# Post-norms by token at four stage boundaries of a two-block transformer kernel, with four weight slots

## The chip, the cores and the metric

The kernel runs on one core of a Trainium2 chip. The metric is the device time of one execution in microseconds (us). The core has TensorE (PE in the profile; PEld is its weight load), VectorE (DVE), ScalarE (ACT) and GpSimd (POOL); SyncE (SP) only sends DMAs. The engines run their own instruction lists in order and meet at semaphores.

## The reference, cut to what matters

512 tokens of width 1024 go through two blocks. The first block is four steps, each with a norm before and a norm after:

```
h = h + 0.5*rmsnorm(swiglu(rmsnorm(h, g1), Wg, Wu, Wd), p1)     # FFN 1, inner width 2816
h = h +     rmsnorm(token_mixer(rmsnorm(h, g2)), p2)            # mixer, ends in y @ w_o
h = h + 0.5*rmsnorm(swiglu(rmsnorm(h, g3), Wg', Wu', Wd'), p3)  # FFN 2
gate = sigmoid(rmsnorm(h, g4) @ w_gate);  e = p @ w_proj        # e has an inner width of 256
h = h +     rmsnorm(gate * e, p4)
rmsnorm(x, g) = x * rsqrt(mean(x*x) + 1e-6) * g                 # mean over the 1024 features
```

The second block starts with `rmsnorm(h, norm_mix_2) @ w_in_2`, then has three mixers (a short convolution, sparse attention with 6 heads, dilated attention with 6 heads), a projection, a gated addition and a last norm.

## The kernel before, in words

**Layout.** `h` lies with features on the partitions: eight tiles `hs[k]` of 128 features by 512 tokens. So do `xh` and `xl`, the operands of the next stage: every factor of a large product is split in a high part (rounded) and a low part (the rest), and a product is three matmuls, `hi*hi`, `hi*lo` and `lo*hi`. `ACT` makes a high part by a copy, `DVE` the low part by a subtraction.

**Weights.** They are read once, in 261 units of mostly 128x1024 numbers (512 KB). SP sends a unit into slot `j % SLOTS` of `raw`; ACT writes `whi` from it (`split_hi`), DVE writes `wlo = raw - whi` (`split_lo`), PE reads `whi` and `wlo`. There are `SLOTS = 3` of each of the three. SP waits for `w_lo` of unit j-3 before it sends unit j. `ahead(n)`, which `along` calls at each unit of a group in ACT's and DVE's lists, splits up to unit n+2 (`AHEAD = 2`).

**Products.** A group (`("ffn1", "gu", g)`, `("v", c)`, `("dv",)` and so on) fills four PSUM banks `G[0..3]`. `gemm` goes unit by unit (two k-tiles), in each unit bank by bank, six matmuls for each. With `by_token` a bank holds 128 tokens by up to 512 features (x is the stationary operand); else it holds 128 features by 512 tokens. One unit is 24 matmuls. `pumps` and `hooks` put small work of other kinds between two banks of a unit: attention steps (`background`) or the sums of a norm.

**A boundary (p1 after FFN 1, p2 after the mixer, p3 after FFN 2, p4 after the gate).** The last group of a stage leaves f with features on the partitions. `post_square` squares the eight tiles on ACT, POOL adds the first four, PE sums over the partitions with a column of ones (`total`, `post_sums`), ACT takes the root and DVE the reciprocal, both write a diagonal matrix (`diagonal`), and PE spreads it over the partitions (`spread`) into bank `X[1]`. Only then can `next_input` run: for each of the eight tiles DVE computes `f = f*gain*X[1]` and `h = h + f`, ACT `xh = h*gain` and a square of h, DVE `xl`. The next group's matmuls for k-tile m wait for `x_lo` of tile m. The pre-norm factor of the next stage is not multiplied into x. It is computed from the squares of h (POOL adds them, `pre_gather`), summed on PE at hook `(6, 0)` of the next stage's first group and applied when the banks are read out. At p3 one unit of another group (`("pp", 0)`) lies between the sums and `next_input`.

**Attention.** In the second block the single-tile units (`tiles_in`) are interleaved with attention steps: after each k-tile pair one `pump`. For pair n of a head and a query block the steps are: PE scores, DVE `score` (maximum), ACT exp, DVE `scale` (multiply by the weight), PE `turn_p` (transposes), ACT and DVE copy into `ptr`, PE `weigh`. In DVE's list the order of a round is copy of n, `score(n + 2)` (in the dilated part n + 4), then after a `yield` `scale(n + 1)`. At the end of a unit DVE's and ACT's lists hold reading out the bank (`store`), activations and the split of the next weight unit.

Of the kernel before, what the change touches and what calls it, by code (L numbers as in the profile page):

```python
# [17 lines left out]
SLOTS = 3  # L18
# [95 lines left out]
def two_blocks(nc, A, out):  # L114
    ctx = ExitStack()
    with ctx:
# [51 lines left out]
        rows, _ = sb("rows", [104, 128], F32)  # L168

# [4 lines left out]
        emb = at("emb", [128, 4, T], F32, ah_o)  # L174
        wsr = at("wsr", [128, 4, 128], F32, bh_o)
        xrow = f[:, :, :].rearrange("p k t -> p (k t)").rearrange("p (i c) -> p i c", i=4)
        vtok = xrow
# [52 lines left out]
        sum_done, spread_done, prep_mm = signal("sum_done"), signal("spread_done"), signal("prep_mm")  # L230
        sgu_done, pooled_done = signal("sgu_done"), signal("pooled_done")
# [5 lines left out]
        pt_act, od_done = signal("pt_act"), signal("od_done")  # L237
# [3 lines left out]
        pt_dve, post_done = signal("pt_dve"), signal("post_done")  # L241
# [53 lines left out]
        for name, c in (("pp", 0), ("pg", 0), ("pg", 1), ("pp", 1)):  # L295
            halves(name, *((A["ple_w_proj"][0], 2) if name == "pp" else (A["ple_w_gate"][0], KD)), 0, (c,))
# [81 lines left out]
        def along(group, tiles, ahead, background=None, pumps=(), hooks=None):  # L378

            first, nk, _ = plan[group]  # L380
            for u in range(0, nk, 2):
# [48 lines left out]
        x0_after = {"p1": "s0", "s1": "p1", "p2": "s1", "s2": "p2", "p3": "s2", "s3": "p3", "p4": "s3", "s4": "p4"}  # L430

        def tensor(pe):
# [3 lines left out]
            def gemm(group, x, tiles, by_token=False, order=None, pumps=(), hooks=None, ks=None):  # L436
                first, nk, wid = plan[group]
                order = order or list(range(tiles))
                for u in range(0, nk, 2):
                    n = first + u // 2  # L440
                    kn = min(2, nk - u)
                    pe.wait_ge(w_lo, n)
                    for ti, m in enumerate(order):
                        for kk in range(kn):
                            hi, lo, key = x[ks[u + kk] if ks else u + kk]
                            wv = [w[:, n % SLOTS, kk * wid:(kk + 1) * wid] for w in (whi, wlo)]
                            if u + kk == 0:
                                for s, v in g_free[m]:
                                    pe.wait_ge(s, v)
                            pe.wait_ge(x_hi, key)  # L450
                            for wi, xv in ((0, hi), (1, hi), (0, lo)):
                                start = u + kk == 0 and wi == 0 and xv is hi
                                stop = u + kk == nk - 1 and xv is lo
                                if xv is lo:
                                    pe.wait_ge(x_lo, key)
                                if by_token:
                                    t = pe.matmul(G[m][:, 0:wid], xv[:, m * 128:(m + 1) * 128], wv[wi], start, stop)
                                else:
                                    t = pe.matmul(G[m][:, :], wv[wi][:, m * 128:(m + 1) * 128], xv, start, stop)
                                if stop:  # L460
                                    t.then_inc(*acc_done.event((group, m)))
                                elif xv is lo and kk == kn - 1 and ti == tiles - 1:
                                    t.then_inc(*unit_read.event(n))
                        if ti in pumps:
                            pump(background)
                        if hooks and (u, ti) in hooks:
                            hooks[u, ti]()
# [9 lines left out]
            def total(st, j, sq, first=False, end=False):  # L477
                if first and st in x0_after:
                    pe.wait_ge(rooted, x0_after[st])
                for i in range(4):  # L480
                    t = pe.matmul(X[0][:, i:i + 1], sq[:, i * 128:(i + 1) * 128], ones[:, 0:1], first and i == 0,
                                  end and i == 3)
                t.then_inc(*sum_done.event((st, j)))

            def spread(st, slot):
                pe.wait_ge(diag_dve, st)
                pe.wait_ge(diag_act, st)
                for i in range(4):
                    t = pe.matmul(X[1][:, i * 128:(i + 1) * 128], ones[:, :], sqs[slot][:, i * 128:(i + 1) * 128], True, True)
                t.then_inc(*spread_done.event(st))  # L490

            def pre_hooks(st):
                def sums():
                    pe.wait_ge(const, "ones")
                    pe.wait_ge(summed, (st, 7))
                    total(st, "acc", acts[3], True, True)

                def factor():
                    spread(st, 0)
                return {(6, 0): sums, (6, 2): factor}  # L500

            def post_hooks(st):
                def sums():
                    pe.wait_ge(summed, (st, 3))
                    total(st, "acc", acts[0], True)
                return {(6, 0): sums}

            def post_sums(st):
                for j in range(4, KD):
                    pe.wait_ge(squared, (st, j))  # L510
                    total(st, j, sqs[j % 2] if j < 6 else acts[j - 5], False, j == KD - 1)
# [25 lines left out]
            def ffn(name, x, st, post, hooks, pumps=(), fill=None):  # L537
                for hf, (g0, g1) in enumerate(GROUPS):
                    for g in range(g0, g1):
                        gemm((name, "gu", g), x, 4, order=[0, 2, 1, 3], pumps=pumps if g else (),  # L540
                             hooks=hooks if g == 0 else None)
                        g_free[:] = [[(scaled, (name, g, m))] for m in range(4)]
                    for c in range(2):
                        gemm((name, "dn", hf, c), HT[name, hf], 4, hooks=post_hooks(post) if hf and c else None)
                        g_free[:] = [[(taken if hf == 0 else f_scaled, (name, hf, 4 * c + m))] for m in range(4)]
                if fill:
                    fill()
                else:
                    post_sums(post)
                    spread(post, 0)  # L550
# [16 lines left out]
            ffn("ffn1", XT["x0"], "s0", "p1", hooks, (3,))  # L567


            for c in range(2):  # L570
                gemm(("v", c), XT["x1"], 4, by_token=True, hooks=pre_hooks("s1") if c == 0 else None)
# [61 lines left out]
            for c in range(2):  # L633
                gemm(("wo", c), AT["y"], 4, hooks=post_hooks("p2") if c else None)
                g_free[:] = [[(f_scaled, ("wo", 4 * c + m))] for m in range(4)]
            post_sums("p2")
            pe.wait_ge(mixed, ("sgu", 6))
            spread("p2", 0)


# [10 lines left out]
            def project():  # L651
                def rest():
                    post_sums("p3")

                def along_it():
                    spread("p3", 0)
                gemm(("pp", 0), PT["p"], 4, hooks={(0, 0): rest, (0, 3): along_it})
                g_free[:] = [[(taken, ("emb", m))] for m in range(4)]

            background.append(embed("p", None))  # L660
            ffn("ffn2", XT["x2"], "s2", "p3", pre_hooks("s2"), (3,), project)


            gemm(("pg", 0), XT["x3"], 4, pumps=(1, 3), hooks=pre_hooks("s3"))
            drain(background)
            g_free[:] = [[(scaled, ("pg", m))] for m in range(4)]
            gemm(("pg", 1), XT["x3"], 4, pumps=(1, 3), hooks=post_hooks("p4"))
            g_free[:] = [[(scaled, ("pg", 4 + m))] for m in range(4)]
            gemm(("pp", 1), PT["p"], 4, pumps=(3,))
            g_free[:] = [[(f_scaled, ("pg", 4 + m))] for m in range(4)]  # L670
            post_sums("p4")
            spread("p4", 0)


            gemm(("dv",), XT["x4"], 4, by_token=True, hooks=pre_hooks("s4"))
# [195 lines left out]
            for t_no, (name, m, n) in enumerate(tiles_in):  # L871
# [6 lines left out]
                for k in range(KD):  # L878
                    hi, lo, key = XT["x4"][k]
# [22 lines left out]
            def sums():  # L902
                pe.wait_ge(summed, ("fin", 3))
                pe.wait_ge(exp_done, (PAIRS - 1, 1))
                total("fin", "acc", acts[0], True)
# [19 lines left out]
        def scalar(act):  # L925
# [19 lines left out]

            def start_hi(k):
# [7 lines left out]
            def pre_square(st, m):  # L954

                if m >= 3:
                    act.wait_ge(summed, (st, m - 2))
                square(st, m, hs[m], sqs[m % 2] if m else acts[3])
# [4 lines left out]

            def diagonal(st):
                act.wait_ge(r_done, st)
                for i in (1, 3):
                    t = act.activation(sqs[0][:, i * 128:(i + 1) * 128], ident[:, :], ACT.Copy, scale=rtok[:, i:i + 1])
                t.then_inc(*diag_act.event(st))
# [5 lines left out]
            def pre_hooks(st):  # L974
                def sums():
                    act.wait_ge(const, "eps")
                    root(st, "acc")
                    diagonal(st)
# [14 lines left out]
            def factors(st):  # L993
                root(st, 7)
                diagonal(st)

            def next_input(st, x, gain, between=None):

                for m in range(KD):
                    act.wait_ge(h_done, (x[m][2][0], m))  # L1000
                    act.activation(x[m][0], hs[m], ACT.Copy, scale=col(gain, m)).then_inc(*x_hi.event(x[m][2]))
                    pre_square(st, m)
                    if m == 0 and between:
# [1184 lines left out]
```

## Time and profile before

| | |
|---|---|
| median of 3 runs (lowest, highest) | 1699.48 us (1697.94, 1704.07) |
| the profiled execution, own time | 1704.4 us |
| its span, first to last instruction | 1702.5 us |
| PE busy | 1631.2 us, 96% |
| PEld, DVE, ACT, POOL busy | 78%, 45%, 34%, 12% |
| mean granted TensorE clock | 0.969 |

PE is busy nearly all the time, but its busy time holds stretches at the lower clock and small matmuls too, so the stretches in which it is not at full work have to be looked up one by one.

### The profile page before, as it was taken

How to read it: one execution, taken by the hardware profiler on the slowest of the kernel's cores; microseconds unless marked ns; L12 is line 12 of the kernel's file. 1: busy time of each engine (PE TensorE's matmuls, PEld its weight loads, DVE VectorE, ACT ScalarE, POOL GpSimd, SP SyncE). 2: the span in 40 equal slices, each digit the busy share in tenths (PEclk: the TensorE clock that was granted, in tenths of full speed). 3: DMA queues.
4: the chain of work that ended last, by engine and by line, in shares of the span. 5: the costliest groups of instructions: out<-in, count | busy, mean ns of one | idle time of the engine just before them, and what ended most of it. 6: DMA issues, size and time to landing. Idle time of an engine off the chain costs nothing.

```text
span 1702.5 us, 19182 instructions
## 1 busy us (share of the span) xinstructions
PE 1631.2 (96%) x7926; PEld 1321.6 (78%) x7926; DVE 765.3 (45%) x1055; ACT 575.7 (34%) x866; POOL 211.3 (12%) x193
## 2 busy tenths in 40 slices
PE   8999999998999999998999999998989998987998
PEld 6778888887888778887888888886878676665787
DVE  5444234437444433447444234427464534555444
ACT  5223222325332332234333223324443413333333
POOL 2311001102023200122111001102040000001100
PEclk9999999998999999997999999998989998998999
DMA  5322333231323223231333333221244221211231
GB/s 162 124 88 98 100 99 99 91 96 62 99 75 100 79 83 99 98 106 49 97 97 100 99 99 94 93 98 38 83 105 100 49 53 25 50 38 37 82 105 50
DMA packets 123605, 144.59 MB, mean 85 GB/s; under 512 B 18768, under 2 KB 86496, under 8 KB 123520
## 3 DMA queue, kind: packets, MB, share of 16 engines
q1 hardware_dynamic: 122096, 138.57, 26.4%
q0 software_dynamic: 1424, 4.82, 1.1%
q8 instruction: 62, 1.02, 0.2%
q14 instruction: 23, 0.19, 0.0%
HBM read 141.26 MB, written 2.10 MB: 84 GB/s over the span
## 4 chain that ended last, share of the span: by engine, by line
PE 89%; DVE 7%; ACT 2%; issue 1%; DMA 0%; SPq 0%; DVEq 0%; ACTq 0%
PE G L57 79%; PE X L57 7%; DVE wlo L69 1%; PE X L60 1%; DVE xl L72 1%; DVE h L69 1%; DVE f L72 1%; PE G L60 1%; ACT whi L63 1%; DVE stat L78 1%; ACT prb L63 0%; DVE prb L75 0%; DMA f<-in_x_dram 0%; DVE tmp_t L69 0%; DVE act_t L69 0%
## 5 line engine op out<-in xcount | busy, mean ns | idle before, releaser
L69 DVE TENSOR_TENSOR wlo<-raw,whi 128x1024 fp32r<-128x1024 f32 (+2 forms) x261 | 320.9, 1232 | 584.1 <-ACT whi L63 583.8
L57 PE MATMUL G<-xh,whi 128*128 128x512 f32 x1304 | 525.9, 403 | 14.9 <-ACT emb L63 3.4
L57 PE MATMUL G<-xl,whi 128*128 128x512 f32 x1304 | 513.8, 394 | 1.5 <-DVE xl L72 1.4
L57 PE MATMUL G<-xh,wlo 128*128 128x512 f32 x1304 | 513.9, 394 | 0.0
L63 ACT ACTIVATE whi<-raw 128x1024 fp32r<-128x1024 f32 (+2 forms) x261 | 270.5, 1039 | 583.1 <-PE G L57 575.9
L57 PEld LDWEIGHTS G<-xh,whi 128*128 128x128 f32 x1304 | 248.9, 191 | 73.0 <-issue 16.8
L57 PEld LDWEIGHTS G<-xl,whi 128*128 128x128 f32 x1304 | 248.2, 190 | 56.9 <-DVE xl L72 3.7
L57 PEld LDWEIGHTS G<-xh,wlo 128*128 128x128 f32 x1304 | 248.9, 191 | 48.0
L57 PE MATMUL G<-ah,whi 128*128 128x512 f32 x448 | 176.6, 394 | 1.1 <-issue 1.1
L57 PE MATMUL G<-al,whi 128*128 128x512 f32 x448 | 174.4, 389 | 0.0
L57 PE MATMUL G<-ah,wlo 128*128 128x512 f32 x448 | 174.3, 389 | 0.0
L69 POOL TENSOR_TENSOR tmp_t<-tmp_t,act_t 128x512 f32<-128x512 f32 x52 | 72.5, 1398 | 590.9 <-ACT act_t L63 482.6
L69 POOL TENSOR_TENSOR act_t<-act_t,sq_t 128x512 f32<-128x512 f32 x50 | 74.6, 1492 | 341.0 <-ACT sq_t L63 339.0
L57 PEld LDWEIGHTS G<-ah,whi 128*128 128x128 f32 x448 | 84.1, 188 | 20.0 <-issue 2.8
L57 PEld LDWEIGHTS G<-ah,wlo 128*128 128x128 f32 x448 | 84.1, 188 | 18.1 <-issue 1.0
L57 PEld LDWEIGHTS G<-al,whi 128*128 128x128 f32 x448 | 84.1, 188 | 17.5
L63 ACT ACTIVATE act_t<-act_t 128x512 f32<-128x512 f32 x81 | 50.6, 632 | 99.8 <-DVE act_t L69 98.6
L57 PE MATMUL G<-bh,whi 128*128 128x512 f32 x192 | 75.4, 393 | 0.0
L57 PE MATMUL G<-bl,whi 128*128 128x512 f32 x192 | 75.2, 392 | 0.0
L57 PE MATMUL G<-bh,wlo 128*128 128x512 f32 x192 | 75.2, 391 | 0.0
L69 DVE TENSOR_TENSOR al<-tmp_t,ah 128x512 fp32r<-128x512 f32 x56 | 43.7, 793 | 47.1 <-ACT ah L63 46.7
L69 DVE TENSOR_TENSOR act_t<-G,rpre 128x512 f32<-128x512 f32 x76 | 51.3, 686 | 17.7 <-PE G L57 17.1
(217 smaller groups left out, 1427.7 us busy)
## 6 DMA issues: line engine op xcount, KB each, us to landing
raw<-in_w_in_dram SPq DMA_DIRECT2D x55, 512.0 KB, 3.6
raw<-in_ffn_w_gate_dram SPq DMA_DIRECT2D x88, 256.0 KB, 2.8
raw<-in_ffn_w_up_dram SPq DMA_DIRECT2D x88, 256.0 KB, 3.1
raw<-in_ffn_w_down_dram SPq DMA_DIRECT2D x44, 512.0 KB, 3.6
raw<-in_w_in_dram SPq DMA_DIRECT2D x12, 384.0 KB, 3.3
raw<-in_w_out_a_dram SPq DMA_DIRECT2D x8, 512.0 KB, 3.6
raw<-in_w_out_b_dram SPq DMA_DIRECT2D x8, 512.0 KB, 3.6
raw<-in_w_o_dram SPq DMA_DIRECT2D x8, 512.0 KB, 3.6
```

What stands on the lines that cost most here:

```text
L57: return self.e.matmul(out, lhs, rhs, start=start, stop=stop) if self.e else Idle()
L60: return self.e.transpose(*a) if self.e else Idle()
L63: return self.e.activation(*a, **kw) if self.e else Idle()
L69: return self.e.tensor_tensor(*a) if self.e else Idle()
L72: return self.e.scalar_tensor_tensor(*a) if self.e else Idle()
L78: return self.e.tensor_reduce(*a, **kw) if self.e else Idle()
```

## The change

At each boundary the last two groups (`dn` of the second half of an FFN, `wo`, `pg` and `pp`) are computed `by_token`, so that f lies with tokens on the partitions: `ft(i, c)`, token block i, feature half c. ACT squares with `accum_out`, so the sum over the features falls out as one number for each token; the root and the reciprocal are 128x1 operations for a token block (`norm_f`), ACT scales feature half 0 and DVE half 1. PE turns the normed blocks (`turn_f`: 32 transposes of 128x128 at a boundary, two token blocks at a time), and DVE adds them to h from PSUM in pieces of 128x256 (`add(k, half)`). The last two units of a stage (`tail`) and the first two of the next (`head`) are each computed as one chunk, so that bank 0 is complete a quarter of the way through the chunk; the turns stand at hooks inside it. The first group of FFN 2, which is not by token, is computed in halves of 256 tokens in its head chunk. `total` and `spread` of the post-norms and the diagonals go; the pre-norm's `spread` stays (its stationary operand is a broadcast of `rtok`) except at s3.

`SLOTS` becomes 4, and `wlo` takes the place of `raw` (the subtraction is in place). SP therefore waits until PE has read unit j-4 (`read_of`) before it sends unit j. The order of `pp` and `pg` changes, and in DVE's attention list `scale(n + 1)` moves ahead of the score step.

```diff
-SLOTS = 3
+SLOTS = 4
-        raw, _ = sb("raw", [128, SLOTS, 1024], F32)
+        raw, raw_o = sb("raw", [128, SLOTS, 1024], F32)
+        wlo = at("wlo", [128, SLOTS, 1024], F32R, raw_o)
-        wlo, _ = sb("wlo", [128, SLOTS, 1024], F32R)
...
-        for name, c in (("pp", 0), ("pg", 0), ("pg", 1), ("pp", 1)):
+        for name, c in (("pg", 0), ("pp", 0), ("pp", 1), ("pg", 1)):
...
+                chunks = [[u] for u in range(0, nk, 2)]
+                if head:
+                    chunks[0:2] = [[0, 2]]
+                if tail:
+                    chunks[-2:] = [[nk - 4, nk - 2]]
+                for chunk in chunks:
+                    halves_ = (0, 1) if len(chunk) == 2 and not by_token else (None,)
+                    parts = [(m, half) for half in halves_ for m in order]
+                    for pi, (m, half) in enumerate(parts):
+                        for u in chunk:
...
+            def turn_f(st, half, banks=(0, 1, 2, 3)):
+
+                for b in banks:
+                    if half:
+                        pe.wait_ge(h_done, (BOUNDARY[st], 2 * b + 1, 0))
+                    for k in (2 * b, 2 * b + 1):
+                        for i in (2 * half, 2 * half + 1):
+                            pe.wait_ge(normed_dve if b > 1 else normed_act, (st, i))
+                            t = pe.transpose(X[b][:, (k % 2) * 256 + (i % 2) * 128:(k % 2) * 256 + (i % 2) * 128 + 128],
+                                             ftok[:, i, k * 128:(k + 1) * 128], ident[:, :])
+                    t.then_inc(*f_turned.event((st, half, b)))
+
+            def tail_hooks(st, u):
+                return {(u, 3, "mid"): lambda: turn_f(st, 0)}
+
+            def head_hooks(st, by_token, hooks):
+                return {**hooks, (0, 1, "mid") if by_token else (0, 3): lambda: turn_f(st, 1, (0, 1)),
+                        (0, 2, "mid") if by_token else (0, 5): lambda: turn_f(st, 1, (2, 3))}
...
+            def norm_f(st, i):      # ACT
+
+                act.wait_ge(squared, (st, 1, i))
+                act.wait_ge(scaled, (st, "bias"))
+                act.activation(rpost[:, i:i + 1], ss1[:, i:i + 1], ACT.Sqrt, bias=bias0[:, i:i + 1],
+                               scale=1.0 / D).then_inc(*rooted.event((st, i)))
+                act.wait_ge(r_done, (st, i))
+                act.activation(ft(i, 0), ft(i, 0), ACT.Copy, scale=rpost[:, i:i + 1]).then_inc(*normed_act.event((st, i)))
...
+                for k in range(4):      # cross, ACT
+                    take(k, 0)
+                last()
+                take(4, 0)
+                take(5, 0)
+                square_h(0, 0)
+                square_h(1, 0)
+                split_hi()
+                for k in range(4):
+                    take(k, 1)
+                take(6, 0)
+                take(7, 0)
+                split_hi()
+                for k in range(4, KD):
+                    take(k, 1)
+                    if k % 2:
+                        square_h(k // 2, 0)
+                for b in range(4):
+                    square_h(b, 1)
+                along(head, 4, ahead, hooks=hooks, start=4)
...
+                    for i in range(2):      # cross, DVE; evict(i) reads bank G[i] out
+                        evict(i)
+                        norm_f(st, i)
+                    evict(2)
+                    add(0, 0)
+                    add(1, 0)
+                    norm_f(st, 2)
+                lo(0, 0)
+                add(2, 0)
...
+            def gather_halves(st, key):      # POOL
+
+                for half in range(2):
+                    for b in range(1, 4):
+                        pool.wait_ge(squared, (key, b, half))
...
+                        pool.tensor_tensor(acc[:, half, 0, :], acc[:, half, 0, :], acc[:, half, b, :],
+                                           ALU.add).then_inc(*summed.event((st, half, b)))
+                    pool.wait_ge(summed, (st, half, 3))
+                    pool.tensor_tensor(acc[:, half, 0, 0:256], acc[:, half, 0, 0:256], acc[:, half, 0, 256:512],
+                                       ALU.add).then_inc(*summed.event((st, half)))
...
                 for n in range(DIL, PAIRS):
                     turn_p(n)
+                    if n + 1 < PAIRS:
+                        scale(n + 1)
                     if n + 2 < PAIRS:
                         score(n + 2)
                     yield
-                    if n + 1 < PAIRS:
-                        scale(n + 1)
                     weigh(n)
                     yield
...
                 if j >= SLOTS:
-                    sp.wait_ge(w_lo, j - SLOTS)
+                    sp.wait_ge(*read_of(j - SLOTS))
```

At p4 (`late = (2, 3)`) ACT's list is: four squares of half 0, sigmoid of blocks 0 and 1, their squares, their roots; `last()` then has sigmoid of blocks 2 and 3, their squares and their roots.

## Rows read from the trace of the kernel before

**Rows 1.** The page: the granted TensorE clock in 40 slices.

```profile
PEclk9999999998999999997999999998989998998999
```

**Rows 2.** Chain of work that ended last, around p1: start us, us, what.

```profile
386.14 3.48 PE X L57 x32
...
397.98 1.69 DVE xl L72
```

**Rows 3.** Stretches of p1 to p4, G matmuls alone: length, PE busy (count), clock, DMA.

```profile
380.00:430.00 50.00, 37.98 (x149) 0.86 0.19 60
764.00:814.00 50.00, 36.13 (x137) 0.83 0.20 64
1143.00:1198.00 55.00, 43.18 (x162) 0.91 0.20 67
1222.00:1262.00 40.00, 23.99 (x103) 0.77 0.18 45
```

**Rows 4.** Chain again: one undisturbed unit of G matmuls.

```profile
577.17 5.46 PE G L57 x24
```

**Rows 5.** Timeline of PE: turns of the input and a matmul behind them; turns of `prow`.

```profile
14.94 1.91 PE L60 MATMUL X<-ident,f 128*128 128x128 f32 x8
...
18.22 0.39 PE L57 MATMUL G<-xh,wlo 128*128 128x512 f32 x1
...
818.87 0.60 PE L60 MATMUL X<-ident,prow 128*128 128x128 f32 x4
```

**Rows 6.** Groups of DVE, ACT and POOL, each form for itself.

```profile
L69 DVE TENSOR_TENSOR wlo<-raw,whi 128x1024 fp32r<-128x1024 f32 x245 | 306.6, 1254 | 557.1 <-ACT whi L63 556.8
L69 DVE TENSOR_TENSOR f<-G,f 128x512 f32<-128x512 f32 x16 | 10.5, 685 | 3.5 <-PE G L57 3.5
L72 DVE SCALAR_TENSOR_TENSOR f<-f,half,X 128x512 f32<-128x512 f32 x16 | 11.8, 739 | 7.9 <-PE X L57 7.9
...
L75 DVE TENSOR_SCALAR f<-h,cols 128x512 f32<-128x512 f32 x8 | 3.9, 487 | 0.3
...
L81 DVE RECIPROCAL rtok<-rtok 128x4 f32<-128x4 f32 x10 | 1.8, 178 | 19.2 <-ACT rtok L63 19.2
...
L63 ACT ACTIVATE whi<-raw 128x1024 fp32r<-128x1024 f32 x245 | 258.0, 1055 | 552.8 <-PE G L57 552.8
L63 ACT ACTIVATE xh<-h,cols 128x512 fp32r<-128x512 f32 x40 | 28.8, 723 | 61.1 <-DVE h L69 49.8 <-DVE h L66 10.7
L63 ACT ACT_TABLE_LOAD x21 | 26.9, 1283 | 4.6 <-DVE cols L66 3.1 <-PE X L57 1.2
...
L63 ACT ACTIVATION_READ_ACCUMULATOR prb<-X,stat 128x1 f32 x60 | 11.7, 196 | 0.0
...
L63 ACT ACTIVATE rtok<-X,eps 128x4 f32<-128x4 f32 x10 | 2.6, 264 | 20.6 <-PE X L57 20.6
...
L69 POOL TENSOR_TENSOR act_t<-act_t,sq_t 128x512 f32<-128x512 f32 x50 | 74.6, 1492 | 341.0 <-ACT sq_t L63 339.0
```

**Rows 7.** DMA issues: KB each, median us from issue to landing.

```profile
raw<-in_w_in_dram SPq DMA_DIRECT2D x55, 512.0 KB, 3.6
```

**Rows 8.** What PE waited for from 1300 to 1590, the attention stretch: us, times, longest.

```profile
PE X L60 <- DVE prb L75: 23.2, 12, 4.4
```

**Rows 9.** Timeline of DVE and PE around the second longest of these waits.

```profile
1445.46 1.23 DVE L69 TENSOR_TENSOR wlo<-raw,whi 128x1024 fp32r<-128x1024 f32 x1 [4.16 <-ACT whi L63]
...
1438.56 0.92 PE L57 MATMUL X<-kvn,qn 64*128 64x256 f32 x8
...
1447.33 0.55 PE L60 MATMUL X<-ident,prb 128*128 128x128 f32 x3 [4.01 <-DVE prb L75]
```

**Rows 10.** Stretches with all of PE's matmuls: clock beside what PE did.

```profile
386.00:390.00 4.00, 3.60 (x33) 1.00 0.04 16
390.00:404.00 14.00, 9.18 (x24) 0.51 0.00 0
1400.00:1590.00 190.00, 165.90 (x1011) 0.92 0.13 37
```

More of the change, by code:

```diff
@@ L376, in two_blocks, with along @@
         GROUPS = ((0, 6), (6, 11))
-        def along(group, tiles, ahead, background=None, pumps=(), hooks=None):
+        def along(group, tiles, ahead, background=None, pumps=(), hooks=None, start=0):
             first, nk, _ = plan[group]
-            for u in range(0, nk, 2):
+            for u in range(start, nk, 2):
                 ahead(first + u // 2)
@@ L434, in tensor, with ready, gemm @@
             g_free = [[] for _ in range(4)]
-            def gemm(group, x, tiles, by_token=False, order=None, pumps=(), hooks=None, ks=None):
+            def ready(signal, key, half):
+                pe.wait_ge(signal, (*key, half) if key[0] in HALVED else key)
+            def gemm(group, x, tiles, by_token=False, order=None, pumps=(), hooks=None, ks=None, head=False, tail=False):
                 first, nk, wid = plan[group]
                 order = order or list(range(tiles))
[L439 to L464, printed above, removed]
-                            pump(background)
-                        if hooks and (u, ti) in hooks:
-                            hooks[u, ti]()
@@ L633, in tensor @@
             for c in range(2):
[L634 to L638, printed above, removed]
+                gemm(("wo", c), AT["y"], 4, by_token=True, tail=c == 1, hooks=tail_hooks("p2", 4) if c else None)
+                g_free[:] = [[(f_scaled, ("wo", c, i))] for i in range(4)]
             def embed(p, load):
@@ L991, in post_square, with ffn @@
                 square(st, j, src, dst)
[L993 to L1003, printed above, removed]
-                        between()
-                    if m == 4:
-                        ahead(split["n"] - split["reach"])
-            def ffn(name, post, hooks, pumps=(), fill=None):
+            def ffn(name, post, gain, head, head_hooks, hooks, pumps=(), first=0):
                 for hf, (g0, g1) in enumerate(GROUPS):
                     for g in range(g0, g1):
-                        along((name, "gu", g), 4, ahead, background, pumps if g else (), hooks if g == 0 else None)
+                        if g or not first:
+                            along((name, "gu", g), 4, ahead, background, pumps if g else (), hooks if g == 0 else None)
                         for p in range(2):
@@ new lines, in gate_by_token, with normed_p4 @@
+            def gate_by_token(c, i):
+                act.wait_ge(acc_done, (("pg", c), i))
+                act.wait_ge(r_done, "s3")
+                act.activation(acts[i], G[i][:, :], ACT.Sigmoid, scale=rtok[:, i:i + 1]).then_inc(*activated.event(("pg", c, i)))
+            def normed_p4(i):
+                act.wait_ge(f_scaled, ("pg", 1, i))
+                square_f("p4", 1, i)
+            for i in range(4):
+                gate_by_token(0, i)
+            along(("pp", 0), 4, ahead)
+            along(("pp", 1), 4, ahead)
@@ new lines, in cross @@
+                add(2, 0)
+                lo(1, 0)
+                add(3, 0)
+                lo(2, 0)
+                lo(3, 0)
+                for i in late:
+                    evict(i)
+                add(4, 0)
+                for i in late:
+                    norm_f(st, i)
+                add(5, 0)
+                lo(4, 0)
+                add(6, 0)
+                lo(5, 0)
+                add(7, 0)
+                add(0, 1)
+                add(1, 1)
+                lo(0, 1)
@@ new lines, in cross @@
+                add(2, 1)
+                lo(1, 1)
+                add(3, 1)
+                lo(2, 1)
+                lo(3, 1)
+                split_lo()
+                lo(6, 0)
+                lo(7, 0)
+                add(4, 1)
+                add(5, 1)
+                lo(4, 1)
+                add(6, 1)
+                lo(5, 1)
+                split_lo()
+                add(7, 1)
+                lo(6, 1)
+                lo(7, 1)
+                along(head, 4, ahead, hooks=hooks, start=4)
```

439 lines of the change are left out of this document (236 added, 203 removed).

## The prediction

> **What bounds the kernel.** I read the granted clock of the page first [rows 1]. TensorE has its full clock but for dips, four of them at the boundaries. So TensorE at full clock is the bound, and the question is what it loses where. The chain of work that ended last says the same: a run of G matmuls, and at p1 a break [rows 2]. There the G matmuls give way at 386.1 to 3.5 us of one-column sums; the wait for the root, the spread and `next_input` follow, and the matmuls run through only once the chain leaves the last `xl`, at 399.7.
>
> To size it I took the stretches around the boundaries with G matmuls alone [rows 3]. An undisturbed unit takes 5.46 us for 24, 0.227 us each [rows 4]. p1: 50 - 149*0.227 = 16.2 us lost. p2: 50 - 137*0.227 = 18.9. p3: 55 - 162*0.227 = 18.2. In p4's stretch some 21 of the 103 are 512 wide and 82 are 384 wide; I estimate the latter by columns at 0.173, so 40 - 4.8 - 14.2 = 21.0. Together 74 us. The clock column of the same rows says how much of it is clock: 50*0.14 + 50*0.17 + 55*0.09 + 40*0.23 = 30 us.
>
> Outside, the attention stretch loses most. PE waits there 12 times, 23.2 us in all, for the multiplication of `prb` [rows 8], and the clock is 0.92 over its last 190 us [rows 10], some 15 us of full speed.
>
> **Boundaries, part by part.** Removed: the wait behind the sums, the spread and the whole-tile updates. Added: 32 turns. Four turns take 0.60 us and the first shows its own length in that, so a turn costs between 0.11 and 0.15 [rows 5]; I take 0.11, 3.5 us a boundary. The pre-norm sums and spread stay, 0.9 us. The 256-column matmuls of p2's head are 96 for 48; between half of 0.227 and the whole (11 us more) I take near half, since a 128-column turn needs only 0.11: 1 us.
>
> Now what PE waits for. Let t=0 be the start of the tail chunk; a bank of it takes 12*0.227 = 2.7 us. The turns of blocks 0 and 1 stand at 3.5 banks, t=9.5. The second head unit has the slot of the unit that PE has just left, so SP sends it only at t=0. Behind that wait stand all later weights. It lands 3.6 us later [rows 7], about 3.9; `whi` 1.06 and `wlo` 1.25 follow [rows 6], and in both lists they stand ahead of the tail's work. So `evict(0)` starts at 6.3, although bank 0 is complete at 2.9. Then 0.69 for the eviction, 0.63 + 0.20 for square and accumulator, 0.26 root, 0.18 reciprocal, 0.49 on DVE: 8.8. DVE does block 1 after that: 0.69, 0.83, 0.26, 0.18, and 0.72 on ACT, with the hops 11.5. PE waits 2.0 us. The rest of the chunk ends near 15. The first `lo` costs 0.8 us in pieces. The turns of blocks 2 and 3 wait for block 3, whose eviction stands behind eight pieces in DVE's list: 0.8 us. Then bank 2 needs `lo(0, 1)`. DVE has by then done 10 adds and 6 subtractions of 256 columns; I take 0.40 each, from 0.74 for 512 less 256/0.96 ns, and their overlap. It is 1.7 us late.
>
> What is late next is the sum of squares. PE stops at hook `(6, 0)`, t=37.6, for `summed`. The last piece of h is there at 32.5, its square at 33.5, and POOL has then four more additions of 1.45 (mean 1.49 [rows 6]) and two of half the width, 0.9 each: 41.3. Wait 3.7 us; every later matmul is behind it. In the kernel before this sum was early, as PE itself was late.
>
> Sum for p1: 2.0 + 0.8 + 0.8 + 1.7 + 3.7 + 3.5 + 0.9 = 13.4 us. p3 the same less a spread, 13.0. p2 one more, 14.4. p4: four squares stand before the sigmoids in ACT's list (2.9 us), and sigmoid and root alternate, so three table loads of 1.28 [rows 6] lie on the path: waits of 5.0, 5.9, 2.0 and, as the next unit is narrower and PE earlier there, 5.9; with 4.4 for turns and sums 23.2. Together 64, against 74 - 30 = 44 before without clock losses.
>
> Clock losses remain. After 386.0 to 390.0, with 33 narrow matmuls, the clock was low for 14 us [rows 10]. A wait of about 4 us in the attention stretch was followed by a dip too. I take two dips of some 3.5 us at half rate for p1 to p3, 3 us each, and 8 for p4: 17. So 81 after against 74 before: **+7 us**. That the turned-on chunks give nothing is the uncertain term; its bounds are nothing late (4.4 us each, 18: -56) and every dip as long as before (64 + 30: +20).
>
> **Attention.** The wait at 1447.33 was 4.01 us [rows 9]. DVE stood 4.16 us at `split_lo` for ACT's `whi`, did it from 1445.46 to 1446.7, and had `scale(n + 1)` behind it. Moved ahead of the score step, the scale needs an exp that is a round old, so it is done before the block. PE then has 0.55 us of turns into X and as much into G [rows 9], scores (0.92 for the eight at 1438.56) and six G matmuls, 1.4, some 3 us in all, until `weigh`, which waits for copies behind the same block. So each wait shrinks by up to 2.9 us: of 23.2 about 15 go, and with the idle stretches gone a third of the 15 us of clock: **-20 us**. Its cost: the maximum comes two multiplications later (0.49 each, the like of `f<-h,cols` [rows 6]), 1.0 us, in a round of which PE fills about 5 us; PE meets it only at the scores of the next round, so nothing. Bounds: -8 (waits move to the copies, clock stays) and -30.
>
> **Slots.** Four slots with a later start: SP sends unit j when PE begins j-3, 16 us before it is needed; landing 3.6, `whi` 1.06 and `wlo` 1.25 make 5.9 [rows 6, 7]. Hidden by two units of matmuls; without that cover each unit would cost up to 5.9. In dq and dk, with 18 matmuls a unit (4.1 us), it is still 12 against 6, more while POOL's loads of `w1s` share the DMA engines: +1. The diagonals (ACT 2, DVE 2 operations each) go: -1 at s0, where the gates wait for `rpre`. Moving `w1s` behind POOL's sums delays it some 10 us, and it is needed 100 us later: 0.
>
> **Sum.** +7 - 20 + 0 = -13. The profiled execution took 1704.4, span 1702.5; it lies 4.9 above the median 1699.5. 1704.4 - 13 = 1691.4, on the median's scale 1686.5; I say **1687 us**.
>
> **A rule that speaks against it.** The rows show that after eight turns of the input, at half rate, the matmul at 18.22 had its full clock [rows 5]: turns among matmuls did not hold the clock down. The Trainium skill ("TensorE: Matmul & The Clock Gate", Part 4, PE-mode transpose) says that transposes don't count as PE-busy and that the full clock doesn't engage for them. By it the sum would be that of rival 3; by the row it is the sum above. The trace speaks against the rule, with one case.
>
> **Rivals.** (1) *The cover works*: the sums of squares and the second head unit are not late. The waits for `summed` go (3.7 + 3.7 + 3.0 + 5.9 = 16) and clock losses shrink from 17 to 4: 1687 - 16 - 13 = 1658. For it: DVE is 45% busy. Against: the order of DVE's list, in which each step is behind the one before.
> (2) *Attention gains little*: the waits move to the copies on ACT, -3 instead of -20: 1704. For it: in the 4.01 us wait ACT was the one that DVE waited for. Against: 2.9 us of PE work lie between.
> (3) *Slower: the clock stays low through the crossing*, from the first turns to the sum of squares. In these 34 us PE has some 19 us of matmuls and 3.5 of turns at full clock; at half 45. That is 13.4 us more than the 22.6 + 9 with waits, four times 54, in place of the 17 assumed: 1687 + 37 = 1724. It decides from 5.5 us more a boundary than my sum.
> (4) *Weights late*: a unit's landing after PE's read does not fit in places where pieces are narrow; 10 units of 2.5 us: 1712.
>
> **Chances.** My forecast 0.52, (1) 0.22, (2) 0.15, (3) 0.07, (4) 0.04. The forecast's own range is 1676 to 1698. The range reaches to (1) and (2): **1656 to 1705**. 0.5%, 8.5 us, is about what can be told from no change. Faster: 0.44 of the first and nearly all of (1), 0.64. Same: 0.08 of the first, most of (2), a little of (1): 0.22. Slower: (3), (4) and a part of (2), 0.14.
>
> **What would show it.** In the profile after: no one-column sums and no spread at the stage ends; 128 turns `X<-ident,f` more; PE waits before them of about 2 us and 0.8 us (5 and 6 at p4), and waits before the one-column sum at hook `(6, 0)` of 3 to 6 us released by POOL or its squares. Loss by the measure of rows 3: 16 to 18 at p1 to p3, near 31 at p4. In attention the row `<- DVE prb` down from 23.2 to below 8, in its place waits for `ptr`. `raw` landings 3.6 us still, and no PE wait for `wlo` in long groups. I am wrong if the boundaries lose under 60 or over 100 us together, or if the `prb` waits stay.

## The result, and the profile after

The changed kernel takes 1671.54 us (median of 4, 1671.21 to 1672.53) against 1701.59 for the kernel before on the same chip (median of 4, 1697.94 to 1704.07): ratio 0.9826, 95% interval 0.9804 to 0.9848, 30 us less. The forecast was 12.5 us less. The direction is right and the time lies in the stated range, but the size is not right: more than twice as much came out. The profiled execution has a span of 1670.8 us, 31.7 below that of before.

**Where the 31.7 us came from.** I laid the two traces over each other by the G matmuls done so far. From the start to p1 the new kernel gains 2.4 us, of which 1.6 are a dip of the clock at 89.7 us that this execution of before had and this one of after had not. The four boundaries give +0.3, +1.2, -2.4 and +1.8: together +0.9. The stretch from there to the gated addition of the second block gives -28.5. The rest is -0.6 inside the mixer, between p1 and p2, and -1.1 at the very end. So nearly the whole gain lies in the attention.

**The page**, granted clock in 40 slices, stands as [rows 1] did, but for the digits at p1, p2 and p3 and one in the attention, each of which is 9 now:

```profile
PEclk9999999999999999999999999999989998999999
```

**What PE waited for from 1300 to 1600 us** (engine, line, what it waited for: us, times, longest), against [rows 8]:

```profile
PE X L57 <- DVE ptr L66: 2.6, 3, 1.1
PE G L57 <- DVE gates L75: 2.1, 1, 2.1
PE X L60 <- ACT sq_t L63: 1.9, 1, 1.9
PE G L57 <- issue: 0.8, 1, 0.8
```

All 12 waits for `prb`, 23.2 us, are gone. In their place stand three for the copies in `ptr`, 2.6 us, of which 0.7 us were there before. **The timeline of DVE** at the place of [rows 9], and behind it that of PE:

```profile
1442.89 1.23 DVE L69 TENSOR_TENSOR wlo<-raw,whi 128x1024 fp32r<-128x1024 f32 x1 [4.17 <-ACT whi L63]
1444.03 0.55 DVE L66 COPY ptr<-G 128x384 f32<-128x384 f32 x1
...
1444.69 0.87 DVE L75 TENSOR_SCALAR prb<-prb,stat,gates 128x384 f32<-128x384 f32 x2
```
```profile
1440.28 0.49 PE L60 MATMUL X<-ident,prb 128*128 128x128 f32 x3
1440.61 0.49 PE L60 MATMUL G<-ident,prb 128*128 128x128 f32 x3
1441.03 1.13 PE L57 MATMUL X<-kvn,qn 64*128 64x256 f32 x8
1442.10 0.28 PE L57 MATMUL X<-mcaus,identb 128*128 128x128 bf16 x2
...
1443.76 0.43 PE L57 MATMUL X<-sq_t,vcs 31*64 31x128 f32 x4
1444.73 0.88 PE L57 MATMUL X<-ptr,vnt 128*64 128x128 f32 x12 [0.54 <-DVE ptr L66]
```

DVE still stands 4.17 us for `whi`. But the turns of `prb` no longer need anything behind that: PE goes on from 1440.28 to 1444.19 with turns, scores, mask, six G matmuls (1442.19 to 1443.76) and the compressed part. That is 3.9 us of cover. Of the 4.01 us 0.54 remain, so 3.5 went: the block in DVE's list now ends some 0.4 us later against PE's own list (3.8 us after PE has reached the turns, where it was 3.4). The stretch of 190 us that answers to the 190 us of [rows 10] (all PE matmuls, then the other engines, clock, DMA):

```profile
1370.00:1560.00 190.00, 185.53 (x1356) 137.00 (x1355) 106.97 (x225) 73.87 (x169) 10.68 (x7) 0.95 0.18 48
```

**The boundaries.** Stretches around p1 to p4 with G matmuls alone, of equal length in both kernels and somewhat longer than those of [rows 3] (length, PE busy and count, PEld, DVE, ACT, clock, DMA). Before:

```profile
372.00:432.00 60.00, 47.33 (x189) 36.52 (x188) 2.67 (x4) 2.53 (x4) 0.89 0.23 70
760.00:820.00 60.00, 45.93 (x180) 34.91 (x179) 5.24 (x8) 0.00 (x0) 0.86 0.20 61
1138.00:1200.00 62.00, 49.25 (x190) 37.40 (x189) 5.04 (x8) 2.04 (x4) 0.92 0.20 68
1210.00:1272.00 62.00, 44.70 (x191) 37.95 (x190) 5.34 (x8) 2.30 (x4) 0.83 0.35 82
```

After:

```profile
364.00:424.00 60.00, 45.68 (x187) 35.55 (x187) 2.73 (x4) 2.75 (x4) 0.94 0.23 63
752.00:812.00 60.00, 46.80 (x224) 38.29 (x223) 3.77 (x6) 0.00 (x0) 0.91 0.20 62
1131.00:1193.00 62.00, 48.21 (x200) 37.90 (x199) 3.62 (x6) 2.75 (x4) 0.94 0.23 71
1204.00:1266.00 62.00, 41.44 (x183) 36.35 (x183) 0.00 (x0) 4.83 (x8) 0.86 0.27 69
```

Taken as in the prediction (0.227 us for 512 columns, 0.173 for 384, of which p4's stretch has 96 in both; the 96 of 256 columns at p2 at half), the loss is 17.1, 19.1, 18.9 and 23.8 us before, 79 in all, and 17.6, 20.0, 16.6 and 25.6 after, 80 in all. The clock column is better and the sum is the same. What fills the time that the clock no longer takes, **the timeline of PE at p1**:

```profile
383.10 1.86 PE L60 MATMUL X<-ident,f 128*128 128x128 f32 x15 [1.55 <-ACT f L63]
...
391.30 0.98 PE L60 MATMUL X<-ident,f 128*128 128x128 f32 x7 [0.61 <-ACT f L63]
...
396.13 1.03 PE L60 MATMUL X<-ident,f 128*128 128x128 f32 x8
...
413.75 1.86 PE L57 MATMUL X<-ones,sqf 128*128 128x1 f32 x8 [5.69 <-POOL sqf L69]
```

The turns come at 0.12 us each, the waits before them are short, and the largest is the one at hook `(6, 0)`. **The chain of work that ended last** leads from ACT's squares through POOL's additions to it, where [rows 2] led through `xl`:

```profile
404.44 0.63 ACT sqf L63
...
405.14 1.30 POOL sqf L69
...
406.51 1.99 POOL sqf L69 x2
...
408.64 2.07 POOL sqf L69
...
410.84 2.07 POOL sqf L69
...
412.97 0.73 POOL sqf L69
...
413.75 1.86 PE X L57 x8
```

Over all four boundaries that wait is 22.2 us (5.69, 4.63, 5.69, 6.18).

### The profile page after: what moved, and what is told of

It reads as the page before. It is cut to its first block, busy times and chain, and to the rows that moved or that the text cites. A ratio compares the mean times of both kernels' runs of the same rounds, so it can differ in the third digit from the quotient of the medians.

```text
span 1670.8 us, 19208 instructions
## 1 busy us (share of the span) xinstructions
PE 1608.3 (96%) x7902; PEld 1308.1 (78%) x7902; DVE 737.8 (44%) x1092; ACT 592.9 (35%) x941; POOL 193.8 (12%) x185
## 3 DMA queue, kind: packets, MB, share of 16 engines
q8 instruction: 62, 1.02, 0.2%
## 4 chain that ended last, share of the span: by engine, by line
PE 86%; DVE 5%; ACT 4%; POOL 2%; issue 1%; DMA 1%; SPq 0%; POOLq 0%; DVEq 0%; ACTq 0%
PE G L57 78%; PE X L57 6%; POOL sqf L69 2%; PE X L60 1%; DVE wlo L69 1%; DVE xl L72 1%; DVE h L72 1%; PE G L60 1%; ACT xh L63 1%; ACT whi L63 1%; ACT f L63 1%; ACT sq_t L63 0%; DMA raw<-in_w_in_dram 0%; ACT L63 0%; DMA f<-in_x_dram 0%
## 5 line engine op out<-in xcount | busy, mean ns | idle before, releaser
L57 PE MATMUL G<-xh,whi 128*128 128x512 f32 (+1 forms) x1256 | 499.9, 398 | 7.7 <-DVE act_t L69 2.9
L57 PE MATMUL G<-xl,whi 128*128 128x512 f32 (+1 forms) x1256 | 490.5, 391 | 0.6 <-DVE xl L72 0.3
L57 PE MATMUL G<-xh,wlo 128*128 128x512 f32 (+1 forms) x1256 | 489.2, 390 | 0.0
L57 PE MATMUL G<-whi,ah 128*128 128x512 f32 x320 | 124.6, 389 | 0.0
L57 PE MATMUL G<-whi,al 128*128 128x512 f32 x320 | 124.5, 389 | 0.0
L57 PE MATMUL G<-wlo,ah 128*128 128x512 f32 x320 | 124.5, 389 | 0.0
L57 PE MATMUL G<-whi,xh 128*128 128x512 f32 (+2 forms) x192 | 75.1, 391 | 1.8 <-ACT xh L63 1.8
L57 PE MATMUL G<-wlo,xh 128*128 128x512 f32 (+2 forms) x192 | 72.8, 379 | 0.0
L57 PE MATMUL G<-whi,xl 128*128 128x512 f32 (+2 forms) x192 | 72.8, 379 | 0.0
L57 PEld LDWEIGHTS G<-whi,al 128*128 128x128 f32 x320 | 60.1, 188 | 12.5
```

What stands on the lines that cost most here:

```text
L57: return self.e.matmul(out, lhs, rhs, start=start, stop=stop) if self.e else Idle()
```

## The experiments

The kernel before had a median between 1700.6 and 1702.6 us beside these runs; each ratio is to the kernel before in the same series. In the diffs, lines stand without their surroundings.

**1. The attention edit alone**, on the kernel before, in both parts:

```diff
+                    if n + 1 < PAIRS:
+                        scale(n + 1)
                     if n + 2 < PAIRS:
                         score(n + 2)
                     yield
-                    if n + 1 < PAIRS:
-                        scale(n + 1)
```

> The kernel before with one edit: in DVE's attention lists scale(n + 1) stands ahead of the score step. Theory A (the order alone gives the attention gain): PE's 23.2 us of waits for prb go to under 3, the stretch from the second block's tiles to its output projection shortens by 25 to 28 us, the time is 1701 - 27 = about 1674. Rival B (four slots are needed, since the split of the next unit is what DVE stands at): the waits fall by a third or less, time 1690 to 1697.

1671.83 us, ratio 0.9828 (0.9813 to 0.9844). The waits for `prb` are gone as in the changed kernel. This one edit has the whole gain.

**2. Four slots alone**, on the kernel before (`SLOTS = 4`, `wlo` in the place of `raw`, `read_of`):

> The kernel before with four weight slots, wlo in raw's place and SP's wait on the read of unit j-4, nothing else. Theory A: no more than 2 us either way (1699 to 1703), prb waits still above 20 us. Rival B: 8 us or more faster, prb waits down by a third. Rival C (later weights cost): slower by 3 us or more, with PE waits for wlo at the boundaries.

1700.59 us, ratio 0.9990 (0.9982 to 0.9999): at most 3 us better, no loss.

**3. The changed kernel with the attention edit taken back** (the diff of 1, reversed):

> The changed kernel with the old order of scale and score in DVE's attention lists; boundaries by token and four slots stay. Theory A: it gives back all of the attention gain, 1671.5 + 27 = 1698, within 0.3% of the kernel before, so the boundaries and slots give 1 to 4 us. Rival B (the boundaries carry the gain, the attention reads faster for another reason): 1680 to 1690.

1700.88 us, ratio 0.9997 (0.9986 to 1.0008). The redesigned boundaries and the slots together are worth nothing that these runs can tell (the interval is 2.4 us faster to 1.4 us slower).

**4. The attention edit in the dilated part alone, in the sparse part alone, and in both with four slots**, on the kernel before:

> The kernel before, with the multiplication moved ahead of the score step in the dilated part of the attention alone. The two parts together gave -31 us. Theory (the gain is that of the 12 waits of 4 us for prb and of the clock behind them): the waits lie mostly in one part; the part that holds them gives nearly all. The waits that I saw lie at 1400 to 1560 us, which is mostly the sparse part, so I expect -3 to -10 here. Rival (each round gains alike): half, -15.

> The kernel before, with the multiplication moved ahead of the score step in the sparse part alone. Theory: -21 to -28, the rest of the 31. Rival (each round alike): -15.

> The kernel before, with the multiplication moved in both parts and with four slots (wlo in the place of raw). If the slots are worth nothing next to the move, 1671 as with the move alone. If the stall that is left in the attention is one for late weights, which four slots cure, 1666.

Dilated: 1700.61 us, ratio 0.9992 (0.9979 to 1.0005). Sparse: 1670.32, 0.9799 (0.9780 to 0.9819). Both with slots: 1670.36, 0.9799 (0.9779 to 0.9820). What PE waited for from 1300 to 1600 in the dilated one:

```profile
PE X L60 <- DVE prb L75: 21.4, 9, 4.4
```

So nine of the twelve waits, 21.4 us, belong to the sparse part, and the gain with them. The three of the dilated part, 1.8 us, are below what these runs can tell, and so is what the slots add to the edit.

**5. The sum of squares, mostly on PE.** On the changed kernel: POOL adds only pieces 1 and 2 of token half 0 to its piece 0, and PE sums all that is left with 24 one-column matmuls instead of four.

```diff
-                        pe.wait_ge(summed, (st, 1))
-                        total(st, "acc", lambda i: acc[:, i // 2, 0, ...], True, True)
+                    for half, bs in ((0, (0, 3)), (1, (0, 1, 2, 3))):
+                        for b in bs:
...
+                                t = pe.matmul(X[0][:, 2 * half + i:2 * half + i + 1], acc[:, half, b, c:c + 128], ones[:, 0:1], ...)
```

> The changed kernel, but POOL adds only the first three square pieces of token half 0; PE sums the other five pieces itself (24 one-column matmuls for 4 at s1 to s4). Theory D (the wait for POOL's seven additions is what takes the boundaries' gain back): the waits of 5.7, 4.6, 5.7 and 6.2 us before hook (6, 0) fall under 2.5, PE pays 20 matmuls of 0.11 = 2.2 us each, the half-rate stretches behind them go (some 13 us at half rate in three or four places): 3 to 6 us a boundary, 12 to 24 in all, 1648 to 1660. Rival E (PE would then wait as long for the squares or the next unit's weights): under 5 us, 1667 or more.

1664.96 us, ratio 0.9790 (0.9769 to 0.9810), 6.6 below the changed kernel. But the five executions lie between 1661.6 and 1670.7, and the profiled one was the slowest of them: laid over the changed kernel's trace it gains 1.5 us at the boundaries. How much of the 6.6 is theirs stays open. The wait is gone and this stands in its place (timeline of PE; then two stretches of all PE matmuls, clock behind POOL's column):

```profile
409.80 6.81 PE L57 MATMUL X<-ones,sqf 128*128 128x1 f32 x48
```
```profile
404.00:414.00 10.00, 10.00 (x64) 8.99 (x62) 5.11 (x6) 5.01 (x8) 0.39 (x1) 0.98 0.41 139
414.00:424.00 10.00, 10.00 (x42) 8.68 (x42) 1.97 (x4) 4.02 (x6) 0.00 (x0) 0.68 0.00 0
```

Each of these matmuls has two records. Up to 413.5 us one starts every 0.11 us, from there on every 0.21: the clock falls in the midst of them. The expectation had taken 0.11 us for a whole matmul, which is the price of one record of two. At p1 PE pays 6.8 us where it waited 5.7 and then spent 1.9 on four sums, and the low clock stays.

**6. The sum of squares, half on DVE.** On the changed kernel: POOL adds token half 0 only, DVE half 1, behind its last `xl`.

```diff
                 lo(7, 1)
+                for b in range(1, 4):
+                    dve.wait_ge(squared, (key, b, 1))
...
+                    dve.tensor_tensor(acc[:, 1, 0, :], acc[:, 1, 0, :], acc[:, 1, b, :],
+                                      ALU.add).then_inc(*summed_dve.event((s_next, 1, b)))
```

> The changed kernel, in which DVE makes the four additions of token half 1 of the sum of squares (three of 128x512, one of 128x256) behind its last xl, and POOL only those of half 0. Theory (the boundary pays for POOL's six additions in a row, 8.6 us from the last squares on): the PE waits before the one-column sums, 5.69, 4.63, 5.69 and 6.18 us, go down to some 1 us each, and the eight sums stay at 1.86 us: -18 us. If the half-rate stretch behind each of them (6.8, 6.8, 6.8, 6.8 us) goes as well, that is up to 13 us more: 1640 to 1654. Rival (as the kernel with 24 sums on PE showed, a wait that goes is paid for in another way): the two splits of weights that stand behind the additions in DVE's list come late, PE waits for wlo instead: 1662 or more.

**1646.00 us**, ratio 0.9678 (0.9654 to 0.9701), 25.5 us below the changed kernel: the fastest version of this study. The sums at p1, and the stretches as above (p1 to p4):

```profile
409.95 1.02 PE L57 MATMUL X<-ones,sqf 128*128 128x1 f32 x8 [1.42 <-issue]
```
```profile
364.00:424.00 60.00, 50.89 (x218) 39.97 (x217) 2.74 (x4) 2.54 (x4) 1.00 0.28 80
746.00:806.00 60.00, 51.84 (x252) 42.36 (x251) 5.22 (x8) 0.00 (x0) 0.97 0.24 72
1118.00:1180.00 62.00, 53.42 (x230) 42.38 (x229) 5.36 (x8) 4.22 (x7) 1.00 0.25 79
1184.00:1246.00 62.00, 44.97 (x202) 39.01 (x201) 0.00 (x0) 4.83 (x8) 0.89 0.36 86
```

By the same measure they lose 10.5, 13.7, 9.8 and 21.3 us, 55 for 80. The wait went from 22.2 to 5.9 us, and with it most of the low clock: it is 1.00 at p1 and p3, and at the four boundaries 17 us lie at half rate instead of 41. The gain of 25 is larger than the 16 us of waits, because the clock came back too.

**7. The second head unit split later** (behind the norms of blocks 0 and 1), alone and together with 6:

```diff
-                        along((name, "dn", hf, c), 4, ahead)
+                        along((name, "dn", hf, c), 4, ahead, last=not (hf and c))
...
                         evict(i)
                         norm_f(st, i)
+                    split_lo()
                     evict(2)
```

> The changed kernel, in which at p1, p2 and p3 ACT's and DVE's split of the second head unit stands behind the norms of token blocks 0 and 1, so that reading out bank 0 no longer waits for that unit's landing. Theory (the order of the lists makes the first turns late): the waits of 1.55, 1.43 and 1.66 us before the first turns go, -4 us, 1667; the next wlo is ready some 3 us later but still before PE has it. Rival (the time is decided by the sum of squares at the end of the crossing, which waits for POOL): the wait before the sums grows by as much as the first one shrinks, 1671.5.

> Both edits together, DVE making half the additions and the late split. If the boundary's waits are independent, the gains add: some 4 us below the kernel with DVE's additions alone. If only the last wait of a crossing counts, it equals the faster of the two.

Alone 1671.91 us, ratio 0.9822 (0.9797 to 0.9846); with 6, 1649.58, 0.9686 (0.9663 to 0.9708). In the first, the wait of 1.55 us before the turns at p1 is gone, PE waits 0.93 us for `xh` behind them, and 5.68 at the sums as before: the chain through POOL decides. In the second there is no POOL chain to decide, and still nothing comes of it that these runs can tell.

**8. Every turn twice**, on the changed kernel:

```diff
-                            t = pe.transpose(X[b][...], ftok[:, i, k * 128:(k + 1) * 128], ident[:, :])
+                            for _ in range(2):
+                                t = pe.transpose(X[b][...], ftok[:, i, k * 128:(k + 1) * 128], ident[:, :])
```

> The changed kernel, in which PE makes each of the 128 turns at the boundaries twice. Theory (a turn costs 0.11 us and leaves the clock where it is): +14 us less what falls into waits for POOL's sums behind them (up to 5 us a boundary for the turns of blocks 2 and 3, 1.8 us each time, 7 in all): 1678 to 1687, and the stretches at the low clock stay where they are. Rival 3 of the prediction (turns do not hold the clock up): a stretch at the low clock follows each doubled group of turns, at least 5 us more a boundary, 1690 to 1710.

1672.38 us, ratio 0.9825 (0.9809 to 0.9841): 0.8 us more, for 128 turns that take 14 us on PE. At p1:

```profile
384.35 3.50 PE L60 MATMUL X<-ident,f 128*128 128x128 f32 x30 [1.34 <-ACT f L63]
...
393.18 1.91 PE L60 MATMUL X<-ident,f 128*128 128x128 f32 x16
...
397.71 1.91 PE L60 MATMUL X<-ident,f 128*128 128x128 f32 x16
...
415.30 1.86 PE L57 MATMUL X<-ones,sqf 128*128 128x1 f32 x8 [4.78 <-POOL sqf L69]
```

The 30 turns in a row come at 0.12 us, full speed to the end. At the boundaries PE idles 7 us less (37.8 to 30.8), and the stretches at half rate there are 34 us long together instead of 41, which is 3.4 us of full speed; the one at p1 alone is longer, 10.2 for 6.8. 14 - 7 - 3.4 is 3.6. Laid over the changed kernel's trace, the boundaries cost 2.7 us more and the rest of the program was 2.5 faster in this execution. The price lay below both theories: most of the turns filled waits.

**9. p4 without table changes**, on the changed kernel:

```diff
-                act.activation(acts[i], G[i][:, :], ACT.Sigmoid, scale=...)
+                act.activation(acts[i], G[i][:, :], ACT.Copy if c else ACT.Sigmoid, scale=...)
```

> The changed kernel, in which the gate's sigmoid of feature half 1 at p4 is left out (a scaled copy stands in its place), so that ACT needs no table change between the two pairs of token blocks; the output differs by that. Theory (the loads of 1.28 us at 1227.85 and 1231.94 lie on the path to the turns of blocks 2 and 3): the wait of 3.3 us there shrinks by 2.6, that at the first turns (3.1 us, load at 1220.24) stays, and the stretch at the low clock behind it (6.8 us, 3.4 of full speed) goes with it: -2.6 to -6 us, 1666 to 1669. Rival (the loads lie beside DVE's work and PE's own): under 1 us, 1671.

1670.62 us, ratio 0.9821 (0.9801 to 0.9840): within what can be told from the changed kernel. The wait of 3.3 us before the turns of blocks 2 and 3 is 1.1, but PE then waits 1.1 for `xh`, which it did not before, and 7.2 instead of 6.2 at the sums. The place was right, the worth was not: what PE no longer waits there it waits further on.

## Why the prediction was right and wrong

The forecast was -13, the two traces lie 31.7 apart. Of the 18.7 between them 8.5 are the attention, 6.1 the boundaries, and 4.1 lie elsewhere, most of it at the start of the program. Two terms of the sum were mis-sized; their mechanisms were right.

**Attention, -20 forecast, -28.5 measured (-30 alone in run 1): the step that failed first.** It said that PE has "some 3 us in all" until `weigh`, so that "each wait shrinks by up to 2.9 us: of 23.2 about 15 go". 21.4 went. The mechanism was right, the cover mis-sized twice. At the wait it was sized on, PE has 3.9 us: 0.75 of turns, 1.2 of scores and mask (I had the 0.92 of a shorter block), 1.6 of G matmuls and 0.4 of the compressed part, which I had left out. And only two of the waits are longer than that. Of the nine in the sparse part (0.83, 4.01, 1.24, 0.84, 1.05, 3.51, 3.26, 4.43, 2.27) the seven up to 3.51 vanish, and 0.54 and 0.99 remain of the other two. Even a cap of 2.9, laid on each of the nine, would have given 17.8, so 15 was not worked out from the list at all. All idle time of PE from 1300 to 1600 went from 29.0 to 7.6 us, -21.4. The clock: 31 us at half rate in the stretch before, 20 after, -5.1, as forecast. That it fits is in part luck. Of the nine other kernels here with both parts of this edit or the sparse one, one has 20 us at half rate in this stretch as well, seven have 14 and one has 10, which makes the clock's share -8.5 in most of them, and the whole gain in the trace of run 1 31.5. Nothing here shows what sets this difference. 2 us of the 28.5 I cannot assign.

**Boundaries, +7 forecast, 0 measured (run 3; +0.9 between the traces): the second step that failed.** After, I had 81 us, and it is 80. Before, I had 74, and over longer stretches it is 79. 2.8 of the 5 us are at p4, whose stretch of 40 us began and ended inside the disturbance. A loss must be measured from steady state to steady state. That 81 is so near is in part luck, as errors cancel: p4 loses 25.6 where near 31 was foreseen, p2 20.0 where at most 18 was. Step by step at p1: turns late by 2.0 foreseen, 1.55 measured; 0.8 for blocks 2 and 3, 0.6; `lo(0, 1)` 1.7, the wait for `xh` 0.9; `summed` 3.7, measured 5.7; turns 3.5, measured 3.9; clock 3, measured 3.4 (6.8 us at half). The 0.8 for the first `lo` is not seen as a wait. The pre-norm's sums and spread cost 1.7 (0.9 for the sums at full clock, 0.8 for the spread) where I had 0.9. The sum is right to a microsecond: 13.4 foreseen without clock, and 1.55 + 0.6 + 0.9 + 5.7 + 3.9 + 1.7 = 14.4; the loss of 17.6 less 3.4 of clock is 14.2. At p4 I foresaw 18.8 of waits (5.0, 5.9, 2.0, 5.9) and there were 12.6 (3.1, 3.3, none, 6.2): the first three came 1.9, 2.6 and 2.0 us shorter than I had laid them out. The three table loads are in the trace, each 1.28 us.

**The wait for `summed` was 2 us longer than foreseen.** Counted from the start of the tail chunk (some 371.8), PE came to the hook some 1.3 us sooner, having waited less on the way, and the sum was ready some 0.7 later. POOL's six additions took 8.6 us, and 1.5 of that is because its last two large ones took 2.05 us each instead of the 1.3 that they take alone. DVE's `wlo` stands beside them (timelines of DVE and then of POOL in the changed kernel; last, DVE in run 6, where POOL is done by then):

```profile
401.29 2.31 DVE L69 TENSOR_TENSOR wlo<-raw,whi 128x1024 fp32r<-128x1024 f32 x1
...
408.12 3.65 DVE L69 TENSOR_TENSOR wlo<-raw,whi 128x1024 fp32r<-128x1024 f32 x2 [3.07 <-ACT whi L63]
```
```profile
401.06 1.45 POOL L69 TENSOR_TENSOR sqf<-sqf 128x512 f32<-128x512 f32 x1 [6.62 <-ACT sqf L63]
```
```profile
409.77 2.35 DVE L69 TENSOR_TENSOR wlo<-raw,whi 128x1024 fp32r<-128x1024 f32 x2
```

Two splits alone take 2.35 us, beside POOL 3.65. The first one began at 401.29, POOL's addition ended at 402.51, and the split ended 1.09 us after that, about its own length. Further on the two alternate: DVE's split ends at 409.57, POOL's addition at 410.69, DVE's next split at 411.77, POOL's next addition at 412.89, each 1.1 us after the one before. Each engine waits for the other. The Trainium skill ("SBUF — State Buffer", "SBUF: two separate sides") says that the two engines share one pair of ports under an exclusive lock for a whole instruction, when the DVE instruction has two inputs in SBUF and the GpSimd instruction reads SBUF; the trace agrees.

**Slots, 0 forecast:** measured between 0 and -3 us. Right.

**The rivals.** (1) *The cover works*, -29 on the boundaries: not this kernel, but run 6 comes near it with 16 instructions moved from POOL to DVE, and gives -25.5. The second head unit is still late there (PE waits 1.44 us before the first turns at p1). My reason against it (the order of DVE's list) was not what decided; it was POOL's list. (2) *Attention gains little*: refuted by run 1. (3) *The clock stays low through the crossing*: refuted. In the changed kernel the clock at p1 is full from the turns at 383.10 to 412.1, and falls while PE waits for POOL (408.06 to 413.75); with twice the turns the low stretches get shorter together. The Trainium skill ("TensorE: Matmul & The Clock Gate", Part 4, PE-mode transpose) says that the full clock doesn't engage for transposes. The trace of run 8 does not agree: 30 of them in a row ran at a granted clock of 1.00. The row that I had set against it beforehand was weaker than I wrote: the eight turns of the input are at half rate by their pace alone (0.24 us each), the granted clock of that stretch is recorded as 1.00. (4) *Weights late*: `raw` lands after 3.7 us (3.6 before), and no wait for it appears at the boundaries. Two waits for `wlo` of before, 1.34 us behind p3 and 2.06 behind p4, are gone; they stay with four slots alone (1.15 and 2.06), so it takes the redesign to remove them.

## What to carry to other kernels

Before a redesign, look for the instruction that stands in an in-order list behind a block that it does not need: one such line, moved up, gave the whole 30 us here, and the redesign of four boundaries nothing. Size such a gain wait by wait, each capped by all the work that PE has until the next thing it needs from that list, and not from the sum of the waits. And when a redesign moves a reduction from "early because PE is late" to "late because PE is early", give its last steps to the engine that is idle then; that was worth 25 us.

## What the runs showed of the hardware

A sum over partitions by a one-column f32 matmul has two records and costs PE 0.22 us at full clock and 0.43 at half. In run 6 the four sums at p1 start a record every 0.11 us (1.02 us for all), in the changed kernel every 0.21 (1.86 us). That is about as much as a 512-column G matmul (0.227), for one column. In a long row of them the clock fell: in run 5 at 413.5 us, 3.7 us after the first of 24 at p1, so that all 24 took 6.81 us; the stretch of 10 us from 414 on has a clock of 0.68. A group of 30 turns, 3.5 us, between matmuls left the clock at full speed (run 8).

An addition of 128x512 took POOL 1.3 us alone and 2.05 beside DVE's 128x1024 subtraction, and that took DVE 1.2 us alone and 2.3 beside POOL's addition.
